# ScalarE issues the key pages of the cached attention on its hardware queue, four pages ahead; GpSimd issues none

## The reference, cut to what matters

```python
past_k = [cache_k[l][page_table].reshape(nbs, past_len, H_A, 2 * DQK_A) for l in range(DEPTH)]
...
def _diff_attn_block(q, k, v, q_pos, k_pos, lam, slopes):
    s = jnp.einsum('bqhmd,bkhmd->bhmqk', q, k).astype(jnp.float32) * (DQK_A ** -0.5)
    dist = (q_pos[:, None] - k_pos[None, :]).astype(jnp.float32)
    s = s - slopes[None, :, None, None, None] * dist
    s = jnp.where(dist >= 0, s, -jnp.inf)
    p = jax.nn.softmax(s, axis=-1)
    a = p[:, :, 0] - lam * p[:, :, 1]
    return jnp.einsum('bhqk,bkhd->bqhd', a.astype(v.dtype), v)
```

## Time and profile before

| | |
|---|---|
| median of 3 runs | 2557.95 us (2556.85 to 2568.91) |
| the profiled execution | 2563.26 us, its span 2561.6 us |
| PE busy | 2233.8 us, 87% of the span |
| ACT busy | 413.4 us, 16% |
| DVE busy | 478.4 us, 19% |
| POOL busy | 89.1 us, 3% |
| key pages | 128 issues of 256 KB, software queue (46.74 MB with the other transfers of GpSimd) |
| value pages | 128 issues of 256 KB, hardware queue |
| cached attention of layer 0, of layer 1 | about 282 to 422 us, about 1165 to 1307 us |

### The profile page before, as it was taken

The page is one execution under the profiler, slowest core; times in us unless marked ns, Lnnn a source line. Parts: engine busy times, 40 slices in busy tenths (PEclk is TensorE's granted clock), DMA queues, the critical chain, the costliest instruction groups (busy, mean ns, idle before and its releaser), DMA issues.

```text
span 2561.6 us, 35629 instructions
## 1 busy us (share of the span) xinstructions
PE 2233.8 (87%) x14217; PEld 1603.7 (63%) x14218; DVE 478.4 (19%) x1155; ACT 413.4 (16%) x864; POOL 89.1 (3%) x165
## 2 busy tenths in 40 slices
PE   6998876778999999978767787999799998989996
PEld 3675554765677666655557656994499647836743
DVE  1043212532100021441134332000100000000002
ACT  1123442111100011234421121000000001001002
POOL 0000230000000000002300000000000000000000
PEclk8799896958999999988968597999899999998998
DMA  9644884013233332367810105877477776996992
GB/s 302 185 130 131 280 305 133 1 38 115 83 129 113 119 101 82 115 200 254 300 43 1 53 17 182 293 259 302 151 259 273 285 267 251 390 400 225 370 381 80
DMA packets 260562, 486.44 MB, mean 190 GB/s; under 512 B 15072, under 2 KB 143788, under 8 KB 260370
## 3 DMA queue, kind: packets, MB, share of 16 engines
q1 hardware_dynamic: 246578, 437.10, 49.3%
q0 software_dynamic: 13792, 46.74, 5.4%
HBM read 474.81 MB, written 8.98 MB: 189 GB/s over the span
## 4 chain that ended last, share of the span: by engine, by line
PE 76%; DMA 8%; DVE 6%; ACT 4%; issue 4%; SPq 1%; POOL 0%; POOLq 0%; DVEq 0%; ACTq 0%
PE ps L713 19%; PE ps L789 16%; PE ps L856 9%; PE ps L755 4%; DMA region<-in_cache_k_dram 3%; PE ps L826 3%; PE ps L900 2%; PE ps L769 2%; PE ps L876 2%; PE ps L999 2%; PE ps L697 2%; PE ps L951 2%; DMA ring<-in_moe_w_down_dram 2%; PE ps L702 1%; PE ps L1080 1%
## 5 line engine op out<-in xcount | busy, mean ns | idle before, releaser
L789 PE MATMUL ps<-region,ring 128*128 128x224 f32 (+1 forms) x2816 | 435.8, 315 | 6.1 <-DMA ring<-in_moe_w_up_dram 6.1
L789 PEld LDWEIGHTS ps<-region,ring 128*128 128x128 f32 x2816 | 423.7, 191 | 26.4 <-issue 24.0
L713 PE MATMUL ps<-hT,ring 128*128 128x320 f32 x1472 | 403.5, 438 | 6.1 <-ACT hT L1381 6.1
L713 PEld LDWEIGHTS ps<-hT,ring 128*128 128x128 f32 x1472 | 283.2, 193 | 125.5 <-ACT hT L1381 6.6
L856 PE MATMUL ps<-ring,big 128*128 128x512 f32 (+1 forms) x528 | 234.7, 600 | 6.1 <-DMA ring<-in_moe_w_down_dram 6.1
L856 PEld LDWEIGHTS ps<-ring,big 128*128 128x128 f32 (+1 forms) x528 | 94.2, 182 | 138.3 <-issue 128.0
L1080 PE MATMUL ps<-C,region 128*128 128x128 f32 x512 | 92.4, 312 | 33.1 <-DMA region<-in_cache_k_dram 31.3
L2142 DVE TENSOR_TENSOR big<-hT,ps 128x896 f32<-128x896 f32 (+3 forms) x24 | 19.8, 827 | 484.6 <-PE ps L789 484.6
L658 POOL DMA_DIRECT2D region<-in_cache_k_dram x128 | 70.4, 550 | 967.3 <-PE ps L1080 929.9
L1080 PEld LDWEIGHTS ps<-C,region 128*128 128x128 f32 x512 | 61.3, 155 | 61.8 <-DMA region<-in_cache_k_dram 47.6
L755 PE MATMUL ps<-big,ring 128*128 128x320 f32 x352 | 95.0, 433 | 1.0 <-DVE big L2116 1.0
(11 more groups left out here) (341 smaller groups left out, 2104.8 us busy)
## 6 DMA issues: line engine op xcount, KB each, us to landing
ring<-in_moe_w_up_dram SPq DMA_DIRECT2D x144, 1024.0 KB, 8.0
ring<-in_moe_w_down_dram SPq DMA_DIRECT2D x80, 1024.0 KB, 9.3
ring<-in_ada_w_dram SPq DMA_DIRECT2D x48, 1024.0 KB, 8.1
region<-in_cache_k_dram POOLq DMA_DIRECT2D x128, 256.0 KB, 4.5
region<-in_cache_v_dram SPq DMA_DIRECT2D x128, 256.0 KB, 4.7
ring<-in_w_in_dram SPq DMA_DIRECT2D x28, 1024.0 KB, 5.5
ring<-in_moe_w_up_dram SPq DMA_DIRECT2D x32, 768.0 KB, 5.6
ring<-in_dense_w_up_dram SPq DMA_DIRECT2D x22, 1024.0 KB, 5.1
```

The source lines that it names most:

```text
L713: m = mm(ps[:, b + o, 0:n], w[:, k, o * P:(o + 1) * P], rhs[:, k, 0:n], start=(first and k == 0), stop=(last and k == nk - 1))
L789: m = mm(ps[:, 2 * part + t // 2, 256 * (t % 2):256 * (t % 2) + n], w[:, kk, t * P:(t + 1) * P], XE[:, k, t0:t0 + n], start=(k == 0 and t ...
```

## The change

The 64 key pages of a layer are no longer issued by GpSimd. ScalarE issues the first four of a layer ahead of its wait for `s_btd`, that is between the norms and the prompt's attention. It issues page n + 4 each time it has seen that page n is transposed, and copies page n after that. The register read of the page's number is now made by ScalarE too, after the wait on `s_kt`. The hardware loop over two of the phases is written out (a Python range), so page numbers are constants. The six stores of GpSimd are no longer behind the key pages.

```diff
@@ gpsimd @@
-                def pages(s):
-                    for p in range(NPG):
-                        pg = pool.value_load(pt_sb[0:1, bass.ds(s * NPG + p, 1)], min_val=0, max_val=NPOOL - 1)
-
-                        if p >= 4 or not isinstance(s, int) or s > 0 or l > 0:
-                            pool.wait_ge(s_kt, 64 * l + s * NPG + p - 3)
-                        pool.dma_start(kring[:, p % 4, :], cache_k[l, bass.ds(pg, 1)].rearrange("o k h d -> (o k) (h d)")
-                                       ).then_inc(s_kf[p % 4], 16)
-
-                pages(0)
-                with pool.Fori(1, NSEQ) as s:
-                    pages(s)
-
@@ scalar, after the norms @@
+                def key_page(n):
+                    pg = act.value_load(pt_sb[0:1, n:n + 1], min_val=0, max_val=NPOOL - 1)
+                    nc.scalar.dma_start(kring[:, n % 4, :], cache_k[l, bass.ds(pg, 1)].rearrange("o k h d -> (o k) (h d)")
+                                        ).then_inc(s_kf[n % 4], 16)
+
+                act.wait_ge(s_pt, 16)
+                if l > 0:
+                    act.wait_ge(s_mB, 3 * l)
+                    act.wait_ge(s_out, 16 * 8 * l)
+                for n in range(4):
+                    key_page(n)
+
                 act.wait_ge(s_btd, l + 1)
@@ scalar, pair_k @@
                         act.wait_ge(s_kt, 16 * g + n + 1)
+                        if 16 * i + n + 4 < NSEQ * NPG:
+                            key_page(16 * i + n + 4)
                         if not (l == 0 and isinstance(i, int) and i == 0 and n < 2):
                             act.wait_ge(s_kmm, 16 * g + n - 1)
                         A(ktb[:, n % 2, :], ps[:, n % 2, :], ACT.Copy).then_inc(s_ktA, 1)
@@ scalar @@
-                pair(0)
-                with act.Fori(1, NPAIR - 1) as i:
+                for i in range(NPAIR - 1):
                     pair(i)
```

## The result

| | before | after |
|---|---|---|
| median | 2560.33 us (2556.83 to 2568.91, 17 runs) | 2574.94 us (2568.56 to 2584.10, 17 runs) |
| ratio | | 1.0050, 95% interval 1.0038 to 1.0062 |
| the profiled execution | 2563.26 us | 2581.38 us |
| key pages' landing, median | 4.5 us | 3.9 us |
| GpSimd busy | 89.1 us | 18.8 us |

The change costs 12.8 us (9.7 to 15.9; 0.5% of 2560.33). The forecast was 28.4. The direction was right and the time lies in the range, but less than half of the cost is there.

The account below looks back on a forecast made before the run. The prediction took a loop of latencies, key pages loaded into four slots, to bound the cached attention, and ScalarE's two-bank loop to replace it. Terms of +14.2 us a layer, +28.4 for both, gave a median of 2586 us, range 2556 to 2626.

Parts of the forecast that it names:

- first four pages, the pause: Between norms and prompt's attention, four issues on ScalarE delay layer 0 by 3.8 us with nothing to cover it; +7.6 in sum.
- key part: Once a layer, eleven pages at 1.46 us instead of 1.28 and later first copies: +2.8 a layer.
- phases without stores: Three phases a layer, each +3.5 us from steady pages, other copies and the start: +10.5 a layer.
- stores: GpSimd's stores go out early, so value pages no longer wait behind them: -2.9 us a layer.
- loop written out: ScalarE's written-out loop saves register additions off the path: taken as 0, bounded by 2.2 us either way.
- The issue: On ScalarE, one page's issue costs 1.10 us, 0.34 of it the issue itself; bounds 0.34 and 2.7.
- The steady pages: In each phase, ten pages bound by ScalarE's two-bank loop take 1.58 us instead of 1.50: +0.8 a phase.
- The starts of phases: At each phase's start, two issues in a row stand on the path: 2 x 1.25 = +2.5 us.
- A: Rival: the load loop stays the later one and hides the issues in steady pages; +11, so 2569 us; chance 0.20.
- B: Rival: ScalarE's issue and copy don't overlap, so each page takes at least 1.85 us; 2620 us; chance 0.15.
- C: Rival: faster, if an issue costs under 0.98 us and landing falls about 1 us; 2528 to 2544 us; chance 0.11.
- D: Rival: ScalarE's and SP's hardware queues hold each other up in the phases; +10, so 2596 us; chance 0.12.

Follow-up runs that it names:

- e9: The kernel before with only ScalarE's hardware loop over two phases written out, GpSimd still issuing the key pages: 2560.39 us, ratio 1.0001.
- e1: The changed kernel, but ScalarE issues a layer's first four pages behind its first square of the norms, where it waits anyway: 2567.47 us, ratio 1.0025 to before.
- e2: The changed kernel, but GpSimd makes the six stores as late as before, behind the key part and phases: 2580.14 us, ratio 1.0083 to before.
- e3: The kernel before, but GpSimd makes a layer's six stores behind its first four key pages instead of all 64: 2552.99 us, ratio 0.9973.
- e4: The kernel before with six register reads on ScalarE where the changed kernel issues its first four pages, no transfer moved: 2567.89 us, ratio 1.0036.
- e11: The kernel before, but GpSimd issues layer 0's first four key pages later, once the first half of the value rows is made: 2554.93 us, ratio 0.9971.
- e12: The kernel before with the edits of e3 and e11, GpSimd still issuing every key page: 2550.16 us, ratio 0.9955.
- e6: e1 with a second register read of the page's number in each issue on ScalarE: 2608.38 us, ratio 1.0192 to before.
- e5: e1 with ScalarE issuing page n + 4 behind its copy of page n instead of ahead of it: 2544.03 us, ratio 0.9942 to before.
- e8: e1 with the edits of e5 and e7, register read ahead of the wait and issue behind the copy: 2533.97 us, ratio 0.9906 to before.
- e7: e1 with the register read of page n + 4 ahead of the wait for page n's transpose: 2540.84 us, ratio 0.9925 to before.
- e10: The changed kernel with the edits of e5 and e7, the first four pages left where the change has them: 2547.45 us, ratio 0.9950 to before.

## Why the prediction was half right

The terms, both layers together, beside what the runs show. "Like kernels" are profiled executions that share the part in question.

| term | forecast | measured | from |
|---|---|---|---|
| first four pages, the pause | +7.6 | +7.9 | 4.50 and 4.63 us against 0.64 twice |
| prompt's attention behind it | 0 | +3.8 | means with and without the pause: 48.8 and 45.5, 48.2 and 47.7 (with e9 in the second: +3.4) |
| key part | +5.6 | +4.6 | after, e1, e2 (26.8 and 26.9) against before, e3, e4, e9, e11, e12 (24.6 and 24.5) |
| phases without stores | +21 | +11 | after, e1 (90.3, 89.5) against e3, e12 (85.4, 83.4) |
| stores | -5.8 | -5.8 | ends of the third phases |
| loop written out | 0 | 0 | e9 |
| start of the kernel | none | -7.4 | e11 |
| sum | +28.4 | +14.1 | as a whole: +12.8 (9.7 to 15.9) |

The forecast was 15.6 us too high. The phases make 10 of it and the start of the kernel 7.4; the clock behind the pause works the other way.

**The pause** was right to 0.3 us. The step "nothing covers it" held. What was left out is that with a gap in PE's work the clock also stayed at 1.2 GHz for longer.

**The issue** was priced at 1.10 us from SP's spacing, and ScalarE took 0.66 + 0.34 = 1.00 from wake to end of issue on the chain above. It lasted 344 ns, 395 at most. The landing time was left alone and fell from 4.5 to 3.9 us. It was shortest in e6, 3.6, where pages come slowest, and 4.2 in e1, e5 and e8 and 4.5 in e7; on the software queue it was 4.5 in before and 4.3 in e3, e11 and e12. The pace of the pages doesn't explain all of it: e1 has after's loop, and e8 is faster than e7.

**The steady pages** are the step that failed: "the ten steady pages at 1.58 instead of 1.50 give +0.8", taken three times a layer, +4.8 in sum. The loop itself was right: in the first two phases of each layer ten pages took 15.6 us as a mean of after, e1 and e2, where 15.8 was forecast. But in the six kernels whose GpSimd issues the pages (before, e3, e4, e9, e11, e12) they took 15.2, not 15.0 (single phases from 14.2 to 17.8), so it is +0.4 each. And in the third phase the last four pages of a layer have no successor, so ScalarE issues nothing ahead of copies 12 to 15, which the condition in the diff says plainly. There ten took 14.1 us against 14.7, -0.6 each. Steady pages in sum: +0.4, not +4.8. (The executions of before and after alone give +0.9.)

**The starts of phases** were the largest term, 6 x 2.5 = 15, with 6 x 0.2 for other copies. In the same nine kernels they took 11.0 us against 8.6, +2.4 each, 14.5 in sum, the other copies within it; two issues of 1.00 in a row make 2.0 of each. The rest of the miss lies in the ends of the first two phases, 3.8 us against 4.25 (-1.8 in sum; in before's layer 0 PE waited there 1.2 us for a value page), and between the phases. From the turned output to the next query blocks ScalarE takes 0.12 us where the loop is written out, in e9 too, and 0.26 to 0.57 in before: -1.1 in sum. That is the written-out loop, which the forecast bounded by 2.2 and took as nothing; e9's time can't tell 1.1 us from none. All four make 14.5 + 0.4 - 1.8 - 1.1 = +12, beside the +11 of the table.

**What was missing** is the start of the kernel, -7.4 us. The prediction followed each moved page forward, into the stretch where it now goes out, and never asked what its old place had cost. The page issues at 19.6 us stood in the earlier trace rows as the start of their range, and it took them for free: "they were out of everybody's way". That after has this gain too is read from its median and from e2 and e10, which start like it (224.9 and 232.4 us); its own profiled execution, with 236.6, doesn't show it. That one was late by PE's pace: its chain waits for no transfer between 19 and 52 us, and sixteen multiplications with the weights' first chunks take longer than in e11, where they take 1.07 (after, chain of waits):

```profile
31.85 1.86 PE ps L938 x16
```

At a granted clock of 0.50 before has the same 1.86 for them, at 57.58 us; the clock's own record of after's execution begins only at 45.5 us. Why the clock was down there stays open. This is probably also why its profiled difference, 18.1, is larger than the 12.8 of all runs.

**The rivals.** *A*, the steady loops hide it: false for the loop (e6), though of its two premises the first held, the landing fell by 0.6. The measured time lies near A's 2569 for other reasons. *B*, no overlap of issue and copy: false; issues run beside a running ACTIVATE. Timeline of ScalarE, after:

```profile
352.89 1.20 ACT L1524 ACTIVATE region<-region,small 128x1088 f32<-128x1088 f32 x1
353.51 0.34 ACTq L1460 DMA_DIRECT2D region<-in_cache_k_dram  x1
...
354.09 0.57 ACT L1520 ACTIVATE region<-ps 128x512 f32<-128x512 f32 x1
...
354.64 0.34 ACTq L1460 DMA_DIRECT2D region<-in_cache_k_dram  x1
```

The issue from 353.51 to 353.85 lies wholly inside the exponential, 352.89 to 354.09, and the next starts when the copy behind it has just ended. *C* named the right condition: e5, e7 and e8 take the issue, the read or both off the path, so under 0.98 us, and are faster than before, by 15 to 24 us. But 11.5 us of that e12 has too, with GpSimd issuing every page, and e5's interval overlaps e12's; only e8's lies clear of it. *D*, two hardware queues that hold each other up: not seen in after. SP's value issues kept 338 ns as a median and 1926 at most (1927 before). 36 of ScalarE's 128 issues overlap one of SP's in time; these took 345 ns as a median and 385 at most, and of all the longest was 395. In the experiments single issues of ScalarE took up to 985 ns (e8), but 10 of the 13 over 400 ns overlap none of SP's. The lock that the Trainium skill describes (Perfetto Trace Analysis, "DMA Instruction — HWDGE (DVE, Sync)") costs some 40 ns an issue at most in after. Its other rule, that issuing from several engines only saves the sequencer's time (DMA: Bandwidth & Descriptors, "Issuing engines are not separate DMA queues"), isn't contradicted, but says half of what happened: here the sequencer's time was moved from an engine that had nothing else to do to one on the path, 1.00 us a page.

## What to carry to other kernels

An issue belongs behind the work that others wait for: one statement moved below the copy turned the change, with its first pages in a gap, from 0.25% slower into 0.6% faster, and its register read belongs ahead of the wait. When a transfer is moved, price its old place as well as its new one, the start of the kernel above all, where early loads for a late stage stand in front of the first weights. And read the edges of a loop, its first and last turns, from the code before multiplying by its count.

## What was unexpected of the hardware

- PE had 1.2 GHz from 242 to 252 us in after, with a gap of 3.81 us in its work, where before, without the gap, had 2.4 (PEclk 0.50 and 1.00); e4, which moves no transfer, had 0.67.
- One megabyte of key pages issued at 19.6 to 23.1 us on the software queue cost 7.4 us of the whole, though the transfer engines moved more in that stretch (360 GB/s from 20 to 40 us in before, 350 in e11). The weights' first chunk on the chain started 1.1 us later and took 1.3 us longer, and PE then worked at 1.2 GHz for 10.2 us, where e11 had 2.4, which is 3.3 us more.
- The same 256 KB load landed in 4.3 to 4.5 us from GpSimd's software queue and in 3.6 to 4.5 from ScalarE's hardware queue (medians of each kernel). Among the kernels with ScalarE's queue it differed by more than between the queues.
